# One layer of a hybrid decoder in float32: the second normalised input turned by VectorE blocks and a round trip through DRAM, instead of by TensorE transposes

## The reference, cut to what matters

```python
merged = gates[:, :, 0] * yr + gates[:, :, 1] * ya
x = x + jnp.einsum('bsd,de->bse', merged, w_out[layer])

pe = jnp.einsum('bsk,kd->bsd', p[layer], w_ple[layer])
pg = jax.nn.sigmoid(jnp.einsum('bsd,de->bse', rms_norm(x, norm_ple[layer]), w_ple_gate[layer]) + b_ple_gate[layer])
x = x + pg * pe
```

## Time and profile before

| | us |
|---|---|
| median of 3 runs (1343.74 to 1344.83) | 1344.05 |
| span of the profiled execution | 1342.2 |
| PE busy | 1331.9 (99%) |
| DVE busy | 781.2 (58%) |
| POOL busy | 531.0 (40%) |
| ACT busy | 507.8 (38%) |

### The profile page before, as it was taken

How to read it: one execution, slowest core, us unless ns; L and a number is a source line. 1 busy time by engine, 2 the same in 40 slices (tenths; PEclk the granted TensorE clock), 3 DMA queues, 4 the chain that set the end, 5 groups by cost and what they waited for, 6 DMA issues and landing times.

```text
span 1342.2 us, 17647 instructions
## 1 busy us (share of the span) xinstructions
PE 1331.9 (99%) x6262; PEld 1104.3 (82%) x6262; DVE 781.2 (58%) x1253; ACT 507.8 (38%) x1282; POOL 531.0 (40%) x500
## 2 busy tenths in 40 slices
PE   9999999999999999999999999999999999999998
PEld 6887888888888888888888888888888888888887
DVE  6799887842779666565665752148512566134323
ACT  7455646542434444344443688311200011223100
POOL 6975424404458334041340632342067317044020
PEclk9999999999999999999999999999999999999999
DMA  6232312322203032120320332376279644122111
GB/s 240 79 102 87 109 56 79 110 100 72 75 12 84 24 92 64 31 83 22 97 58 30 114 98 88 100 237 220 94 275 412 198 126 157 55 79 63 40 47 47
DMA packets 84823, 139.51 MB, mean 104 GB/s; under 512 B 10464, under 2 KB 41472, under 8 KB 84736
## 3 DMA queue, kind: packets, MB, share of 16 engines
q10 hardware_dynamic: 40288, 75.82, 16.0%
q1 hardware_dynamic: 44448, 62.56, 15.6%
HBM read 108.84 MB, written 29.51 MB: 103 GB/s over the span
## 4 chain that ended last, share of the span: by engine, by line
PE 92%; DVE 5%; issue 1%; ACT 1%; DMA 0%; POOL 0%; SPq 0%; POOLq 0%; DVEq 0%; ACTq 0%
PE bank L1275 28%; PE bank L1280 28%; PE bank L1279 28%; PE bank L1432 2%; PE bank L1412 2%; PE bank L1399 1%; PE bank L1421 1%; DVE xc L1012 1%; PE bank L1525 1%; PE bank L1320 0%; DMA gain_mix<-in_gain_mix 0%; ACT L750 0%; DVE ibuf L1039 0%; DVE qkr L1116 0%; DVE ibuf L1028 0%
## 5 line engine op out<-in xcount | busy, mean ns | idle before, releaser
L549 POOL TENSOR_TENSOR ring<-raw,ring 128x512 fp32r<-128x512 f32 x221 | 310.5, 1405 | 727.1 <-PE bank L1280 642.8
L1275 PE MATMUL bank<-hn,ring 128*128 128x512 f32 x640 | 251.8, 393 | 1.4 <-DVE sgbuf L1000 1.2
L1280 PE MATMUL bank<-hn,ring 128*128 128x512 f32 x640 | 249.4, 390 | 0.0
L1279 PE MATMUL bank<-hn,ring 128*128 128x512 f32 x640 | 249.2, 389 | 0.0
L1275 PE MATMUL bank<-ring,hn 128*128 128x512 f32 x576 | 232.6, 404 | 0.2 <-POOL ring L549 0.2
L1280 PE MATMUL bank<-ring,hn 128*128 128x512 f32 x576 | 225.8, 392 | 0.0
L1279 PE MATMUL bank<-ring,hn 128*128 128x512 f32 x576 | 225.2, 391 | 0.0
L553 POOL TENSOR_SCALAR ring<-raw 128x512 fp32r<-128x512 f32 x221 | 183.5, 830 | 7.9 <-DMA raw<-in_w_rnn_s 7.8
L1275 PEld LDWEIGHTS bank<-hn,ring 128*128 128x128 f32 x640 | 120.2, 188 | 26.7 <-DVE sgbuf L1000 1.6
L1280 PEld LDWEIGHTS bank<-hn,ring 128*128 128x128 f32 x640 | 120.1, 188 | 25.3
L1279 PEld LDWEIGHTS bank<-hn,ring 128*128 128x128 f32 x640 | 120.3, 188 | 24.0
(11 more groups left out here) (181 smaller groups left out, 2153.7 us busy)
## 6 DMA issues: line engine op xcount, KB each, us to landing
raw<-in_w_tail_s SPq DMA_DIRECT2D x104, 256.0 KB, 2.7
g_in<-gate_dram ACTq DMA_DIRECT2D x48, 256.0 KB, 4.4
raw<-in_w_rnn_s SPq DMA_DIRECT2D x45, 256.0 KB, 2.6
raw<-in_w_qkv_s SPq DMA_DIRECT2D x48, 192.0 KB, 2.5
gate_dram<-g_out ACTq DMA_DIRECT2D x32, 256.0 KB, 2.1
raw<-in_w_qkv_s SPq DMA_DIRECT2D x48, 128.0 KB, 2.2
o_dram<-o_buf ACTq DMA_DIRECT2D x48, 128.0 KB, 1.8
o_in<-o_dram ACTq DMA_DIRECT2D x12, 512.0 KB, 3.5
```

The lines of the kernel that those rows point to most:

```text
L549: nc.gpsimd.tensor_tensor(ring[:, ring_slot(p), 1], raw[:, p % RAW], ring[:, ring_slot(p), 0].bitcast(F32), ALU.subtract).then_inc(w_ready, 1)
L1275: ins = T.matmul(out, lhs[0], rhs[0], start=first, stop=False)
L1279: T.matmul(out, lhs[0], rhs[1], start=False, stop=False)
L1280: return T.matmul(out, lhs[1], rhs[0], start=False, stop=last)
```

## The change

- The eight PE transposes per tile (64 in all) and their calls are removed.
- On DVE, step `t` scales in two halves of 512 channels, with the gain read from PSUM banks 4 and 5, and then transposes `xg[t % 2]` in place in blocks of 32 by 32 (one instruction, 128 by 1024). ACT copies the gain into the two banks once, before the steps.
- SP gets `turn_xg(t)`: four DMAs write `xg[t % 2]`, 32 partitions each, to a DRAM buffer in runs of 32 numbers (128 bytes); SP waits for all four, then for the low part of tile `t-1` (`xgT_lo_done`, since there is one `xgT` buffer), and issues one DMA that reads the 512 KB back into `xgT` in runs of 128 numbers, now turned. `xgT` takes the place of `gain_ple`.
- High and low parts are made from `xgT` with a lag of three tiles, in one instruction each over 1024 columns.
- DVE waits in step `t >= 2` for the writes of tile `t-2` (`xg_out`) before it overwrites the buffer.
- SP's weight loads are cut up: up to P7, then `turn_xg(0)`, then the loads of P8 to P11, then `turn_xg(1)` to `turn_xg(7)`, then P12 to P19.

```diff
+            def turn_xg(t):
+                squares = xgt_dram[t % 2]
+                sp.wait_ge(xg_done, t + 1)
+                if t >= 2:
+                    sp.wait_ge(xgT_in, 16 * (t - 1))
+                for i in range(QUADS):
+                    sp.dma_start(squares[:, :, i].rearrange("b i j -> i b j"),
+                                 xg[t % 2][i * QUAD:(i + 1) * QUAD].rearrange("p (b j) -> p b j", j=QUAD)
+                                 ).then_inc(xg_out[t % 2], 16)
+                sp.wait_ge(xg_out[t % 2], 16 * QUADS * (t // 2 + 1))
+                if t == 0:
+                    sp.wait_ge(gain_set, 2)
+                else:
+                    sp.wait_ge(xgT_lo_done, t)
+                sp.dma_start(xgT[:], squares.rearrange("(k b) i a j -> (b i) k (a j)", b=QUADS)
+                             ).then_inc(xgT_in, 16)
+
+            load_pieces(RAW, FIRST_PG + RAW)
+            for t in range(NT):
+                if t < 2:
+                    load_pieces(FIRST_PG + RAW * (t + 1), FIRST_PG + RAW * (t + 2))
+                turn_xg(t)
+            load_pieces(FIRST_PG + 3 * RAW, PIECES)
...
+            for eh in range(2):
+                nc.scalar.activation(bank[4 + eh][:], gain_ple[:, eh * HALF:(eh + 1) * HALF],
+                                     ACT.Copy).then_inc(gain_set, 1)
+
             def xgT_hi(t):
-                act.wait_ge(xgT_done, t + 1)
-                for b in range(2):
-                    nc.scalar.activation(m_hi[:, 4 * b:4 * b + 4, t * P:(t + 1) * P],
-                                         bank[4 + b][:].rearrange("p (k q) -> p k q", k=4),
-                                         ACT.Copy).then_inc(xgT_hi_done, 1)
+                act.wait_ge(xgT_in, 16 * (t + 1))
+                nc.scalar.activation(m_hi[:, :, t * P:(t + 1) * P], xgT[:], ACT.Copy).then_inc(xgT_hi_done, 1)
...
                     if t >= 2:
-                        xgT_lo(t - 2)
-                    if t >= 2:
-                        dve.wait_ge(xgT_done, t - 1)
-                    V.scalar_tensor_tensor(xg[t % 2][:], x2[t][:], rstd_x[:, t:t + 1], gain_ple[:],
-                                           ALU.mult, ALU.mult).then_inc(xg_done, 1)
+                        dve.wait_ge(xg_out[t % 2], 16 * QUADS * (t // 2))
+                    for b in range(2):
+                        bs = slice(b * HALF, (b + 1) * HALF)
+                        ins = V.scalar_tensor_tensor(xg[t % 2][:, bs], x2[t][:, bs], rstd_x[:, t:t + 1], bank[4 + b][:],
+                                                     ALU.mult, ALU.mult)
+                    link(ins)
+                    V.transpose(xg[t % 2][:], xg[t % 2][:]).then_inc(xg_done, 1)
+                    if t >= LAG_XG:
+                        xgT_lo(t - LAG_XG)
...
-            def xg_transposes(t):
-                pe.wait_ge(xg_done, t + 1)
-                if t >= 1:
-                    pe.wait_ge(xgT_lo_done, 2 * t)
-                for k in range(KD):
-                    ins = T.transpose(bank[4 + k // 4][:, (k % 4) * P:(k % 4 + 1) * P], xg[t % 2][:, k * P:(k + 1) * P], ident[:])
-                ins.then_inc(xgT_done, 1)
```

More of the change, by code:

```diff
@@ L35 @@
 CLASSES = (1, 4, 8)
+QUAD = 32
+QUADS = P // QUAD
 OFF_Z_RNN = RNN
@@ L54 @@
 FIRST_O = FIRST_TAIL + PIECES_Z
+FIRST_PG = PIECES - 2 * (KD + KP)
 def ring_slot(p):
@@ L110 @@
 P_CUT = (2, 4)
+LAG_XG = 3
 WARM = 16
@@ L313, in build_layer @@
         gain_ple = at("gain_ple", [P, D], F32, X + 45056)
+        xgT = at("xgT", [P, KD, P], F32, X + 45056)
         pT = at("pT", [P, KP, S], F32, H + 40960)
@@ L341, in build_layer @@
         gate_dram = nc.dram_tensor("gate_dram", (2 * KD, P, S), F32, kind="Internal").ap()
+        xgt_dram = nc.dram_tensor("xgt_dram", (2, D // QUAD, QUAD, QUADS, QUAD), F32, kind="Internal").ap()
         stat_dram = nc.dram_tensor("stat_dram", (2, TILES, P), F32, kind="Internal").ap()
@@ L442, in build_layer @@
         xg_done = sem("xg_done")
-        xgT_done = sem("xgT_done")
+        gain_set = sem("gain_set")
+        xg_out = [sem("xg_out0"), sem("xg_out1")]
+        xgT_in = sem("xgT_in")
         xgT_hi_done = sem("xgT_hi_done")
@@ L502, in _, with load_pieces @@
             sp.dma_start(spare_first[:, :, 0], chunk_bias(0).rearrange("p (q i) -> p q i", q=4)).then_inc(bq_in[0], 16)
[L504 to L512, removed]
-                else:
-                    load(p % RAW, a["w_tail_s"][p - FIRST_TAIL])
+            def load_pieces(first, end):
+                for p in range(first, end):
+                    sp.wait_ge(w_ready, p + 1 - RAW)
+                    if p < FIRST_QKV:
+                        load(p % RAW, a["w_rnn_s"][p])
+                    elif p < FIRST_TAIL:
+                        c, k = divmod(p - FIRST_QKV, KD)
+                        for u, col, width, dst in chunk_sources(c):
+                            sp.dma_start(raw[:, p % RAW, dst:dst + width], a["w_qkv_s"][u * KD + k, :, col:col + width]
+                                         ).then_inc(raw_in[p % RAW], 16)
+                    else:
+                        load(p % RAW, a["w_tail_s"][p - FIRST_TAIL])
@@ L913, in _ @@
             act.dma_start(bias_ple[:], a["bias_ple"].to_broadcast([P, D])).then_inc(bple_in, 16)
-            def xgT_hi(t):
-                act.wait_ge(xgT_done, t + 1)
-                for b in range(2):
-                    nc.scalar.activation(m_hi[:, 4 * b:4 * b + 4, t * P:(t + 1) * P],
-                                         bank[4 + b][:].rearrange("p (k q) -> p k q", k=4),
-                                         ACT.Copy).then_inc(xgT_hi_done, 1)
+            act.wait_ge(gain_in, 16)
+            act.wait_ge(stat_set, 1)
+            for eh in range(2):
+                nc.scalar.activation(bank[4 + eh][:], gain_ple[:, eh * HALF:(eh + 1) * HALF],
+                                     ACT.Copy).then_inc(gain_set, 1)
+            def xgT_hi(t):
+                act.wait_ge(xgT_in, 16 * (t + 1))
+                nc.scalar.activation(m_hi[:, :, t * P:(t + 1) * P], xgT[:], ACT.Copy).then_inc(xgT_hi_done, 1)
             for t in range(NT):
@@ L929, in _ @@
                                      scale=1.0 / D).then_inc(x2_std, 1)
-                if t >= 2:
-                    xgT_hi(t - 2)
+                if t >= LAG_XG:
+                    xgT_hi(t - LAG_XG)
             for i in range(2 * NT + 1):
@@ L936, in _ @@
                     nc.scalar.activation(fin[i % 3][:], fin[i % 3][:], ACT.Sigmoid).then_inc(pg_done, 1)
-                if i < 2:
-                    xgT_hi(NT - 2 + i)
+                if i < LAG_XG:
+                    xgT_hi(NT - LAG_XG + i)
                 if i >= 1:
@@ L1204, in xgT_lo @@
             def xgT_lo(t):
[L1205 to L1210, removed]
+                dve.wait_ge(xgT_hi_done, t + 1)
+                V.tensor_tensor(m_lo[:, :, t * P:(t + 1) * P], xgT[:], m_hi[:, :, t * P:(t + 1) * P].bitcast(F32),
+                                ALU.subtract).then_inc(xgT_lo_done, 1)
             for i in range(2 * NT):
@@ L1225, in _ @@
                     if t == 0:
-                        dve.wait_ge(gain_in, 16)
+                        dve.wait_ge(gain_set, 2)
                     dve.wait_ge(x2_std, t + 1)
@@ L1244, in _ @@
                     V.tensor_tensor(fin[i % 3][:], bank[n % 4][:], bias_ple[:, hs], ALU.add).then_inc(pre_done, 1)
-                if i < 2:
-                    xgT_lo(NT - 2 + i)
+                if i < LAG_XG:
+                    xgT_lo(NT - LAG_XG + i)
                 if i >= 1:
@@ L1535, in _ @@
                 natural(n, lambda k: (m_hi[:, k, ts], m_lo[:, k, ts]), first + eh * KD, KD, t == NT - 1)
[L1536 to L1539, removed]
             first += 2 * KD
@@ L1548, in _ @@
                 if eh == 0:
-                    pe.wait_ge(xgT_lo_done, 2 * t + 2)
+                    pe.wait_ge(xgT_lo_done, t + 1)
                 if i == 0:
@@ L1555, in _ @@
                 natural(n + 1, lambda k: (pT_hi[:, k, ts], pT_lo[:, k, ts]), p0 + KD, KP, t == NT - 1)
-                if eh == 0 and t < 2:
-                    xg_transposes(NT - 2 + t)
 def blocks(w, col):
```

## The result

The changed kernel takes 1387.19 us (median of 4 runs, 1386.18 to 1387.61) against 1344.39 us for the kernel before in the same session: ratio 1.0317, 95% interval 1.0303 to 1.0332. It is 3.2% slower. The forecast was 1389.0 us. The profiled execution has a span of 1385.1 us, 42.9 us above that of before.

What follows compares the result with a forecast made beforehand. PE, busy 99%, bounds the kernel. To its 1342.2 us span add 34.2 (tile 2 of stage P later, 7.0 us of transposes included), 9.3 (waits), 1.5 (clock): 1387.2; plus 1.85 for the median, 1389.0 us; range 1368 to 1422.

Steps and rivals of the forecast that it cites:

- one round: From DVE's step 3 on, per tile: issue 0.4, fixed 1.6, read 1.7, writes 4.0, DVE 4.0; sum 11.7 us.
- slow clock behind the last wait: After PE's last wait in stage P, matmuls run at 1.2 GHz until the clock is back: 0 to 6 us, taken 1.5.
- The start: On SP, P11's load waits for POOL's low part of P7, holding tile 1's writes until 1218.9, their data ready before 1196.
- only the loop: Rival: P11's load does not hold SP, step 3 ends 21.5 us earlier, 1367.5 us; chance 0.07.
- The loop: Closed ring from step 3: DVE's low part, SP's read, next writes, DVE's scaling; 11.7 us per tile against PE's 5.44.
- short runs are dear: Rival: tile writes in 128-byte runs take 5.9 to 7.5 us, entering about 6.5 times, 1401 to 1412 us; chance 0.22.
- the doubling: For the 128-byte writes, 2 x 11.6 ns per run from the read-modify-write rule: writes 5.9 us, a round 13.6 us.
- its upper price: Upper bound for a tile's writes in short runs, from a load's extra runs: 7.5 us, adding 23 us, 1412 us.
- The waits inside stage P: PE waits 8.5 us in the middle of tile 2 for tile 0's product, then 0.8 us more for tile 7: 9.3 us.
- the slow bank: First bank of a stage P tile at the lower clock, 10.9 us instead of 5.45, still under a round.
- The 0.8 us at tile 3: Further PE wait in stage P, for tile 7's low part: 22.3 us against 21.5 us, 0.8 more.
- two gates in a row: SP held by P11's load until 1218.5, then the closed loop of 11.7 us per tile from step 3 on.

Runs made afterwards that it cites:

- The first experiment: Changed kernel with only SP's order altered, the load of P11 behind all eight turned tiles: 1367.64 us, ratio 1.0169 to the kernel before.
- the third experiment: Changed kernel with the four writes per tile in rows of 4096 bytes instead of 128-byte runs, output not the reference's: 1379.53 us, ratio 1.0260.

## Why the prediction was right

The sum of the prediction, term by term, against the trace of the changed kernel:

| term | predicted | measured |
|---|---|---|
| writes of tile 1 issued | 1218.9 | 1219.36 |
| DVE's end of step 3 | 1229.2 | 1228.7 |
| one round | 11.7 us | 11.1, 11.0, 12.2, 11.3 us |
| tile 2 of stage P starts, against before | +34.2 us | +32.6 us |
| waits after it | 8.5 + 0.8 us | 6.0 + 0 us, and 2.0 us of slow clock in front |
| slow clock behind the last wait | 1.5 us | 2.0 us |
| block transpose | 1.2 us | 1.25 us |
| span | 1387.2 us | 1385.1 us |

**The start** was the step that mattered most, and it was read off two rows of the trace of before, where it cost nothing: POOL's idle time of 30.75 us and SP's silence until 1222.88. The first experiment gives 19.6 us for it; the rival "only the loop" had worked out 21.5 us as its share. As a separate rival, that case is out: the trace has the wait.

**The loop** was right as a mechanism, shown by the lag of two. The read and writes together took 7.2 us from the issue of the read to the landing of the writes (1228.80 to about 1236.0), predicted 7.7, and DVE's part with its hand-overs 3.9 us, predicted 4.0. But the 7.2 us are made up otherwise than in the sum. It gave SP's issuing of the four writes nothing; in the trace that takes 4.15 us, and the writes land 3.1 us after the last of them begins to be issued. The data moves meanwhile. Which of the two, issue or data, holds the other back is not shown. The writes alone can be seen once, in the DMA queues from 1190.3 to 1194.9, where nothing else moves:

```profile
q1 hardware_dynamic: 4160, 0.52, 70.2%
```

That is 70.2% of 16 engines for 4.6 us over 4160 packets, 12.4 ns for each, beside the 11.6 ns of the earlier trace rows; 3.2 us of data where 4.0 was taken. The row of small packets was the right one, and the addition on top of it was too much. The rival that short runs are dear falls: the doubling that it took would have needed some 23 ns, its upper price more. In the third experiment the same writes in rows of 4096 bytes, also by themselves (1189.5 to 1193), read:

```profile
q1 hardware_dynamic: 192, 0.52, 56.7%
```

That is 2.0 us of 16 engines against 3.2 us for the same bytes in short runs, and 1.6 us less per round. So short runs do cost more here, and only the size that the prediction gave it falls.

The Trainium skill (DMA: Bandwidth & Descriptors, Specifications) gives 512 bytes as the least transfer for line rate, with a read-modify-write below. The traces agree that runs below that size move more slowly, 3.2 against 2.0 us; whether a read-modify-write is behind it no run here shows, and the doubling was the prediction's estimate, not the page's figure.

**The waits inside stage P.** The prediction had 9.3 us for them, and they came as 6.0 us of wait plus 2.0 us that the first bank of tile 2 took longer at the lower clock. The prediction had said that the slow bank hides, and it did, inside that wait; but it had put the whole bank at the lower clock, 10.9 us, and it took 7.4 us (1275.09 to 1282.5), since the clock came back within it. The 0.8 us at tile 3 did not come.

**The clock.** This is PE's clock by stretch in the changed kernel (last three numbers: granted clock, DMA share, GB/s):

```profile
1270.00:1275.00 5.00, 0.00 (x0) 0.00 (x0) 4.36 (x5) 0.02 (x1) 0.00 (x0) 0.50 0.00 0
1290.00:1292.00 2.00, 2.00 (x6) 1.51 (x6) 0.00 (x0) 0.62 (x1) 0.00 (x0) 0.50 0.62 178
1294.00:1296.00 2.00, 2.00 (x11) 1.64 (x10) 1.72 (x2) 0.25 (x1) 1.68 (x1) 1.00 0.51 196
```

While PE waits, the granted clock is at 0.50, 1.2 GHz. After the last wait, which ends at 1288.68, it stays there at first and is at 1.00, 2.4 GHz, from 1294 on. In the chain in order of time the first matmuls take 0.43 us each instead of 0.23:

```profile
1288.68 0.79 PE bank L1315
1289.47 0.43 PE bank L1319
```

Nine or ten matmuls are slow. By the starts in PE's timeline, the 30 from 1288.68 to 1297.52 take 8.84 us, where at 0.227 us each they would take 6.8: the loss is 2.0 us, 5% of the whole.

That the sum came out within 2.1 us is in part luck, with errors of both signs: the start of tile 2 was put 1.6 us too late, the time lost inside stage P 1.3 us too high (9.3 for 6.0 + 2.0), the slow clock behind it 0.5 us too low, and the round of 12.16 us, 1 us of it unforeseen, made up for rounds that were otherwise shorter than predicted. The structure, two gates in a row and a wait inside stage P, is what the runs confirm; the single terms are good to about 1 us.

## What to carry to other kernels

Before a wait is put into a queue, list what the queue already holds around that place and what each entry waits for, not only what the new entry waits for: a load whose lateness cost nothing held seven tiles back by 20 us. When a buffer is handed round between engines, draw the ring of waits and add up its length; more lag is not more slack if it puts a DMA and the work that depends on it into the same ring. A way round a saturated engine can gain no more than what it takes off that engine, here 7 us; a new route with a round of 7.2 us against PE's 5.4 us has to be started early and kept off the queue of the weights before it pays at all.

## What the runs showed that was not expected

Issuing a DMA is not a fixed 0.4 us. In the changed kernel the 32 issues of the writes take 334 to 2522 ns each, with a median of 616; four of them take 2.26 us with nothing just ahead of them, 4.15 us behind the read, and 1.94 us behind the read with long runs; in the first experiment, behind the read and three loads, 5.59 us. So the time grows with the runs and with what was issued just before, and whatever stands behind such a group on SP waits as well. That SP is held by what the queue has still to take in would fit this; no run tests it by itself.

The writes below 512 bytes ran at 12.4 ns per packet of 128 bytes, with all 16 engines at work, close to the 11.6 ns of the few small packets in the trace of before.
